# Values projected feature-major and transposed, last window rows staged in the product ring, and the last two down steps of every block taken token tile by token tile

## The chip, the cores and the metric

The kernel runs on one core of a Trainium2 chip. The metric is the device time of one execution in microseconds. Before the change it is 3422.22 us, the median of three runs (3419.22 to 3426.93). One further execution was profiled: 3422.57 us, with a span from its first to its last instruction of 3420.8 us. All times inside the kernel come from that execution.

## The reference, cut to what matters

One layer of a hybrid streaming encoder runs over a prompt of 2048 rows of width 1024 and over 32 further rows of a running stream (the sample):

```
h = rmsnorm(x, g_pre_mix)
[q | k | v | u_a | u_b | gate logits] = h @ w_in      # v: 2 heads of 64 = 128 columns
u = u_a * sigmoid(u_b)
attn = window attention (own chunk of 64 and two before, 16 query heads, 2 key/value heads, sinks, bias)
conv = silu(layernorm(causal depthwise conv of width 31 over u)) @ w_conv_out
m = sigmoid(g0) * attn + sigmoid(g1) * conv
x = x + rmsnorm(m @ w_out, g_post_mix)
h = rmsnorm(x, g_pre_ffn)
x = x + rmsnorm((silu(h @ w_gate) * (h @ w_up)) @ w_down, g_post_ffn)   # inner width 2816
```

Outputs are x for both streams, the last 128 rows of k and v of each stream, and the last 30 rows of u of each. All data is fp32. Every product of two fp32 operands is made of three matmuls of rounded parts: hi\*hi, hi\*lo and lo\*hi.

## The kernel before, in words

The prompt is cut into four **blocks** b of 512 tokens. The last block, where `ext(b)` holds, also carries the 32 sample rows, so it has 544 columns (two pieces of 272) and five token tiles in place of four. A block is a list of NS = 124 **steps** (`KINDS`), each with one 128x1024 weight tile in two parts: 16 GLU steps (0 to 15), 8 of q (16 to 23), k (24), v (25), 16 gates (26 to 41, `S_A` = 26), 8 of the convolution's projection (42 to 49), 8 of the output projection (50 to 57), 44 of the FFN (58 to 101) and 22 of the down projection (102 to 123, `S_D` = 102). `G(b, s)` numbers the steps over all blocks. TensorE goes through the steps in order and counts `w_used` up after each. Each other engine has its own loop over b and s in which step s mostly handles the result of step s - 1 (`r = s - 1`).

**Weights.** Rings of 3 slots for the high parts and 4 for the low parts are filled by the SyncE queue (SP). `load_hi(g)` waits until step g - 3 is used, `load_lo(g)` until step g - 4 is. In block 0 the parts are made on the spot (`split_hi` on ScalarE, `split_lo` on VectorE) and stored for the later blocks. SP's program is one ordered list: `weights_at`, then stores and loads of activations at fixed steps.

**Matmul forms.** `feature_major` holds a 128x128 weight tile and streams 512 tokens (24 matmuls; 48 of 272 tokens in the last block); its result is features by tokens. `token_major` with `token_products` holds a tile of tokens and streams 512 features. The v step has a form of its own, `values_of` (L830 to L843): it holds the tokens and streams the 128 value columns, in 96 matmuls of 128 columns (120 in the last block), so that values come out tokens by features, as `times_values` wants them. ScalarE then writes `v_hi` (L1241 to L1245) and VectorE `v_lo` (L1604 to L1610). In the last block VectorE also adds the high and low parts of the last keys and values into `kwin` and `kwin_s` (L1613 to L1622), which lie where `tmp` and `rs_bc` do; SP stores them at step 28 (`S_A + 2`, L603 to L608) and VectorE waits for these stores (L1639) before the layer norm.

**Convolution.** VectorE takes most taps (`conv`, L1388), accumulating in PSUM banks 4 to 7. For three channel tiles ScalarE makes products into the ring `prod` and GpSimd adds them (L692). Both start in a new block only when the previous block's rows are stored (`y_out`), since y shares memory with `x1`. After the taps come `channel_means` (L910), VectorE's subtraction of the mean (L1644), ScalarE's squares (L1261), `channel_squares` (L920) and the scaling (L1659). In blocks 1 to 3 the means follow step 26 and the squares step 27; in block 0 this lies three steps later. The attention units start at step 31 (34 in block 0). The probabilities' parts `pt_hi`, `pt_lo` share memory with `prod`.

**Down steps and the end of a block.** `f_hi` and `f_lo` have two slots. ScalarE makes the high part of down step dd when step dd - 2 is used (L1334 to L1336), VectorE the low part after it (L1756), and TensorE waits for `flo_ok`. After the last step ScalarE takes the squares of the second half of each token tile (`post_squares`, L1101 and L1113), GpSimd makes 1/rms (`post_inv_rms`, L662 to L665), and VectorE runs `residual` (L1435, L1440), which counts `pn_ok`. `store_y` issues one store of the block's rows when the last tile is done: in blocks 0 to 2 at SP's step 1 of the next block, in the last block at the very end, with a second store for the sample. At step 1 of the last block TensorE waits for the previous block's residual of tile 3, because that block uses banks 2 and 3 there.

The order within the down steps is set in TensorE's loop:

```
pe.wait_ge(flo_ok, b * FT + dd + 1)
token_major(b, s, S_D, f_hi[:, dd % 2], f_lo[:, dd % 2], (0, 1), HALF_D,
            range(tiles(b)))
```

## Time and profile before

| what | value |
|---|---|
| median of 3 runs | 3422.22 us (3419.22 to 3426.93) |
| profiled execution: time, span | 3422.57 us, 3420.8 us |
| TensorE busy | 3293.7 us, 96% |
| TensorE weight loads (beside the matmuls) | 2778.7 us, 81% |
| VectorE busy | 1551.4 us, 45% |
| ScalarE busy | 1062.5 us, 31% |
| GpSimd busy | 476.2 us, 14% |
| mean granted TensorE clock | 0.983 |
| data moved | 623.30 MB, 182 GB/s |

A matmul's listed duration is that of one from start to end, and neighbours overlap; what a step costs is the distance between starts. PE is TensorE, PEld its weight loads, DVE VectorE, ACT ScalarE, POOL GpSimd, SP SyncE. A wait in square brackets is the engine's idle time before the instruction and what released it.

### The profile page before, as it was taken

What the parts mean: (1) busy time and instruction counts of PE and PEld (TensorE: products, weight loads), DVE (VectorE), ACT (ScalarE), POOL (GpSimd) and SP (SyncE); (2) the same over time, 40 slices, a digit from 0 to 9 for tenths busy, and PEclk for the clock granted to TensorE, in tenths of its full rate; (3) what the DMA queues carried; (4) which work ended last, traced back from release to release, by engine and by line L of the source; (5) the groups of instructions that cost most, each with busy time, mean ns of one, the idle gap of its engine ahead of it and who ended that gap; (6) DMA issues with size and microseconds to landing.
All of it is one profiled execution on the core that took longest, in us unless ns stands there. A gap on an engine that the chain in (4) does not pass through costs nothing.

```text
span 3420.8 us, 43119 instructions
## 1 busy us (share of the span) xinstructions
PE 3293.7 (96%) x17118; PEld 2778.7 (81%) x17118; DVE 1551.4 (45%) x2779; ACT 1062.5 (31%) x1924; POOL 476.2 (14%) x515
## 2 busy tenths in 40 slices
PE   7999989999999999999999999999999998999997
PEld 6778768878787878888787888888898997899985
DVE  6966755544775541013695542003495555200012
ACT  3655432234345421003254421003153532200021
POOL 2830000000460000000280000000074000100000
PEclk9999999999999999999999999999999999999998
DMA  7764367777543355555553354555553322455542
GB/s 233 281 219 163 148 249 283 288 279 285 209 173 123 111 196 174 195 197 198 206 188 124 111 185 173 185 196 199 194 177 126 111 94 85 160 173 173 173 148 106
DMA packets 177895, 623.30 MB, mean 182 GB/s; under 512 B 20592, under 2 KB 28080, under 8 KB 177184
## 3 DMA queue, kind: packets, MB, share of 16 engines
q1 hardware_dynamic: 176736, 620.15, 51.6%
q8 instruction: 136, 2.23, 0.3%
q14 instruction: 63, 0.52, 0.0%
q10 hardware_dynamic: 960, 0.40, 0.0%
HBM read 481.13 MB, written 139.44 MB: 181 GB/s over the span
## 4 chain that ended last, share of the span: by engine, by line
PE 79%; DVE 3%; ACT 1%; DMA 1%; issue 1%; POOL 0%; SPq 0%; DVEq 0%; ACTq 0%; POOLq 0%
PE PS L747 49%; PE PS L801 6%; PE PS L803 6%; PE PS L802 6%; PE PS L783 2%; PE PS L873 2%; DVE PS L1388 1%; PE PS L861 1%; PE PS L920 1%; PE PS L862 1%; PE PS L863 1%; PE PS L890 1%; PE PS L891 1%; PE PS L731 1%; PE PS L892 1%
## 5 line engine op out<-in xcount | busy, mean ns | idle before, releaser
L747 PE MATMUL PS<-h_hi,w_hi 128*128 128x512 f32 (+1 forms) x3288 | 1053.6, 353 | 23.4 <-DVE u L1597 14.9
L747 PE MATMUL PS<-h_hi,w_lo 128*128 128x512 f32 (+1 forms) x3288 | 1054.6, 354 | 0.0
L747 PE MATMUL PS<-h_lo,w_hi 128*128 128x512 f32 (+1 forms) x3288 | 1043.6, 350 | 0.0
L747 PEld LDWEIGHTS PS<-h_hi,w_hi 128*128 128x128 f32 x3288 | 580.3, 189 | 106.4 <-issue 20.6
L747 PEld LDWEIGHTS PS<-h_lo,w_hi 128*128 128x128 f32 x3288 | 579.6, 189 | 89.7 <-issue 1.7
L747 PEld LDWEIGHTS PS<-h_hi,w_lo 128*128 128x128 f32 x3288 | 579.9, 189 | 80.9
L692 POOL TENSOR_TENSOR y<-y,prod 128x512 f32<-128x512 f32 (+1 forms) x333 | 407.9, 1251 | 228.4 <-ACT prod L1154 217.6
L1388 DVE SCALAR_TENSOR_TENSOR PS<-u,dw,PS 128x512 f32<-128x512 f32 (+1 forms) x604 | 434.4, 772 | 7.0
L1748 DVE TENSOR_TENSOR f<-PS,tmp 128x512 f32<-128x512 f32 (+1 forms) x88 | 61.6, 700 | 669.0 <-PE PS L747 650.2
L801 PE MATMUL PS<-w_hi,f_hi 128*128 128x512 f32 x748 | 297.4, 398 | 5.8 <-DVE f L1748 5.4
L803 PE MATMUL PS<-w_hi,f_lo 128*128 128x512 f32 x748 | 295.2, 395 | 0.0
L802 PE MATMUL PS<-w_lo,f_hi 128*128 128x512 f32 x748 | 294.0, 393 | 0.0
L1251 ACT ACTIVATE tmp<-PS 128x512 f32<-128x512 f32 (+1 forms) x88 | 52.9, 601 | 675.0 <-PE PS L747 655.7
L662 POOL TENSOR_TENSOR prs<-pss 128x1 f32<-128x1 f32 x34 | 11.1, 326 | 1790.7 <-ACT tmp L1113 1790.7
L1154 ACT ACTIVATE prod<-u,dw 128x512 f32<-128x512 f32 (+1 forms) x333 | 229.5, 730 | 34.5 <-POOL y L692 34.1
L1043 ACT ACTIVATE w_hi<-w_raw 128x1024 fp32r<-128x1024 f32 x124 | 131.3, 1059 | 349.9 <-DVE w_raw L1527 109.4
L1533 DVE TENSOR_TENSOR w_lo<-w_raw,w_hi 128x1024 fp32r<-128x1024 f32 x124 | 162.2, 1308 | 165.4 <-ACT w_hi L1043 164.9
L1756 DVE TENSOR_TENSOR f_lo<-f,f_hi 128x1024 fp32r<-128x1024 f32 (+1 forms) x88 | 109.1, 1240 | 271.3 <-ACT f_hi L1336 271.3
L1459 DVE CUSTOM_DVE_ANT_0 p<-PS,bias,sink_sb 128x256 f32<-128x256 f32 x272 | 115.6, 481 | 145.5 <-PE PS L873 141.9
L1336 ACT ACTIVATE f_hi<-f 128x1024 fp32r<-128x1024 f32 (+1 forms) x88 | 93.8, 1070 | 262.8 <-PE PS L803 262.8
L801 PEld LDWEIGHTS PS<-w_hi,f_hi 128*128 128x128 f32 x748 | 141.0, 189 | 38.6 <-DVE f L1748 7.0
L803 PEld LDWEIGHTS PS<-w_hi,f_lo 128*128 128x128 f32 x748 | 140.8, 188 | 33.4
(185 smaller groups left out, 4001.0 us busy)
## 6 DMA issues: line engine op xcount, KB each, us to landing
w_lo<-lo_dram SPq DMA_DIRECT2D x372, 512.0 KB, 4.5
w_hi<-hi_dram SPq DMA_DIRECT2D x372, 512.0 KB, 3.6
w_raw<-in_w_stream SPq DMA_DIRECT2D x124, 512.0 KB, 4.0
hi_dram<-w_hi SPq DMA_DIRECT2D x124, 512.0 KB, 4.1
lo_dram<-w_lo SPq DMA_DIRECT2D x124, 512.0 KB, 4.0
x<-in_x_prompt SPq DMA_DIRECT2D x4, 2048.0 KB, 11.4
out_y_prompt<-x SPq DMA_DIRECT2D x4, 2048.0 KB, 7.1
xs<-in_x_prompt SPq DMA_DIRECT2D x12, 512.0 KB, 5.5
```

The lines of the kernel that those rows point to most:

```text
L692: nc.gpsimd.tensor_tensor(y[:, ct, 0:yw], y[:, ct, 0:yw], prod[:, n % RING, 0:yw], ALU.add).then_inc(prod_used, 1)
L747: last = nc.tensor.matmul(PS[:, k0 + off, 0:n], w, x[:, k, c0:c0 + n], start=first and k == 0, stop=stop and k == KT - 1)
L801: nc.tensor.matmul(out, hi, wk[0], start=first, stop=False)
L802: nc.tensor.matmul(out, hi, wk[1], start=False, stop=False)
L803: return nc.tensor.matmul(out, lo, wk[0], start=False, stop=last_k)
L1043: A(w_hi[:, g % HI, :], w_raw[:, g % LO, :], ACT.Copy).then_inc(w_hi_ok, 1)
L1154: A(prod[:, n % RING, 0:yw], u[:, ct, k:k + yw], ACT.Copy, scale=dw[:, ct, k:k + 1]).then_inc(prod_ok, 1)
L1336: A(f_hi[:, dd % 2, :, 0:c], f[:, 2 * kp:2 * kp + 2, 0:c], ACT.Copy).then_inc(fhi_ok, 1)
L1388: ins = STT(out, src, dw[:, ct, k:k + 1], acc(b, ct), ALU.mult, ALU.add)
L1459: nc.vector.tensor_tensor_reduce(out=p[:, h, :], in0=PS[:, 2 + h // 2, (h % 2) * 2 * P:(h % 2 + 1) * 2 * P], in1=bias[:, head, :], scale=1 ...
L1533: TT(w_lo[:, g % LO, :], w_raw[:, g % LO, :], w_hi[:, g % HI, :].bitcast(F32), ALU.subtract).then_inc(w_lo_ok, 1)
L1756: TT(f_lo[:, dd % 2, :, 0:c], f[:, 2 * kp:2 * kp + 2, 0:c], f_hi[:, dd % 2, :, 0:c].bitcast(F32), ALU.subtract).then_inc(flo_ok, 1)
```

## The change

Three parts. **Values:** step 25 becomes a `feature_major` step. ScalarE copies its result to `tmp[:, 1]` (new semaphore `v_sb_ok`); after step 26 (`turn_step`) TensorE turns it by one 128x128 transpose per token tile into banks 6 and 7 (`turn_values`, `vt_done`), and `v_hi` and `v_lo` are made from there, one step later than before. In the last block the transposes stand behind the wait for all taps, ahead of the means. TensorE's step 27 waits for `v_sb_ok`, and the squares for `v_lo`. **Windows:** `kwin` and `kwin_s` move to the memory of the product ring. VectorE writes them once all products are used, one step later; the wait for their stores moves from VectorE's layer norm to ScalarE's second attention unit. SP's step for the stores stays 28. **Down steps:** `down_tail` takes steps 122 and 123 together, for each token tile both; each tile but the last counts `d_done`, and `post_squares` waits for its tile alone. Both steps' `w_used` come with the last tile. In the last block `store_y` makes one store per token tile. Shown without unchanged surroundings:

```diff
 ckv = at("ckv", R_pt, [P, 2, P])
-kwin = at("kwin", R_sc, [P, 2, P])
-kwin_s = at("kwin_s", R_sc + 2 * P * 4, [P, 2, P])
+kwin = at("kwin", R_pt, [P, 2, P])
+kwin_s = at("kwin_s", R_pt + 2 * P * 4, [P, 2, P])
 assert top[0] <= nc.sbuf_usable_end, (top[0], nc.sbuf_usable_end)
...
 o_done, w_gain_ok = sem("o_done"), sem("w_gain_ok")
+d_done = sem("d_done")
...
 kv_hi_ok, hist_ok = sem("kv_hi_ok"), sem("hist_ok")
+v_sb_ok, vt_done = sem("v_sb_ok"), sem("vt_done")
 dve_chain, pool_chain, act_chain = sem("dve_chain"), sem("pool_chain"), sem("act_chain")
...
+
+def turn_step(b):
+
+    return S_A
...
     def store_y(b):
-        m = post_tile(b, tiles(b) - 1, 1)
-        sp.wait_ge(pn_ok, m + 1)
+        if ext(b):
+            for tt in range(4):
+                sp.wait_ge(pn_ok, post_tile(b, tt, 1) + 1)
+                r0 = b * T + tt * P
+                sp.dma_start(y_prompt[r0:r0 + P, :], x1[:, tt, :]).then_inc(y_out, 16)
+            sp.wait_ge(pn_ok, post_tile(b, 4, 1) + 1)
+            sp.dma_start(y_sample, x1[SR:P, 4, :]).then_inc(y_out, 16)
+            return
+        sp.wait_ge(pn_ok, post_tile(b, tiles(b) - 1, 1) + 1)
         sp.dma_start(y_prompt[b * T:(b + 1) * T, :].rearrange("(t p) d -> p t d", p=P),
                      x1[:, 0:4, :]).then_inc(y_out, 16)
-        if ext(b):
-            sp.dma_start(y_sample, x1[SR:P, 4, :]).then_inc(y_out, 16)
...
                 sp.dma_start(u[:, :, HIST + T:UW - S], state).then_inc(state_in, 16)
-            if ext(b) and s == S_A + 2:
+            if ext(b) and s == turn_step(b) + 2:
                 sp.wait_ge(win_ok, 4)
...
     store_y(NB - 1)
-    sp.wait_ge(y_out, 16 * (NB + 1))
+    sp.wait_ge(y_out, 16 * (NB - 1 + 5))
     sp.wait_ge(win_out, 16 * 8)
...
             result_out(pe, b, s - 1)
-        result_out(pe, b, s - 2)
+        if s == S_A + 1:
+            pe.wait_ge(v_sb_ok, b + 1)
+        else:
+            result_out(pe, b, s - 2)
         for k in range(KT):
...
-    def values_of(b, s):
-
-        g, k0 = G(b, s), zbank(b, s)
-        weights(g)
-        result_out(pe, b, s - 2)
+    def down_tail(b):
+
         for tt in range(tiles(b)):
-            t0, out = tok0(b, tt), PS[:, k0 + tt // 4, (tt % 4) * P:(tt % 4 + 1) * P]
-            for k in range(KT):
-                hi, lo = h_hi[:, k, t0:t0 + P], h_lo[:, k, t0:t0 + P]
-                wk = [w[:, g % n, k * P:(k + 1) * P] for w, n in ((w_hi, HI), (w_lo, LO))]
-                nc.tensor.matmul(out, hi, wk[0], start=k == 0, stop=False)
-                nc.tensor.matmul(out, hi, wk[1], start=False, stop=False)
-                last = nc.tensor.matmul(out, lo, wk[0], start=False, stop=k == KT - 1)
-        last.then_inc(w_used, 1)
+            for s in (NS - 2, NS - 1):
+                dd = s - S_D
+                if tt == 0:
+                    weights(G(b, s))
+                    pe.wait_ge(flo_ok, b * FT + dd + 1)
+                for kk in range(2):
+                    last = token_products(b, s, S_D, f_hi[:, dd % 2], f_lo[:, dd % 2], (0, 1), HALF_D,
+                                          kk, tt)
+                if tt == tiles(b) - 1:
+                    last.then_inc(w_used, 1)
+            if tt < tiles(b) - 1:
+                last.then_inc(d_done, 1)
+
+    def turn_values(b):
+
+        pe.wait_ge(v_sb_ok, b + 1)
+        for tt in range(tiles(b)):
+            last = nc.tensor.transpose(PS[:, 6 + tt // 4, (tt % 4) * P:(tt % 4 + 1) * P],
+                                       tmp[:, 1, tok0(b, tt):tok0(b, tt) + P], ident_sb[:])
+        last.then_inc(vt_done, 1)
...
             if s < first_unit(b):
-                if s == S_A - 1:
-                    values_of(b, s)
-                elif b or s >= 2:
+                if b or s >= 2:
                     feature_major(b, s, h_hi, h_lo, groups(b))
+                if s == turn_step(b):
+                    if ext(b):
+                        pe.wait_ge(conv_step, taps_before(b + 1))
+                    turn_values(b)
                 ln = s - S_A - ln_shift(b)
...
                 if ln == 3 and ext(b):
-                    pe.wait_ge(conv_step, taps_before(b + 1))
                     channel_means(b, ypieces, (0, 2, 4, 1, 3, 6, 7, 5), True, True)
                 if ln == 4:
+                    result_out(pe, b, S_A - 1)
                     channel_squares(b, ypieces)
...
                     pe.wait_ge(hf_ok, first_norm(b + 1, tiles(b + 1) - 1) + 1)
+                if s >= NS - 2:
+                    if s == NS - 1:
+                        down_tail(b)
+                    continue
                 pe.wait_ge(flo_ok, b * FT + dd + 1)
...
             if kind == "v":
-                zv = PS[:, zbank(b, r), :].rearrange("p (t a d) -> p t a d", t=4, a=2)
+                A(over(b, tmp[:, 1, 0:c]), z(b, r), ACT.Copy).then_inc(v_sb_ok, 1)
+            if r == turn_step(b):
+                act.wait_ge(vt_done, b + 1)
                 if ext(b):
-                    zw = PS[:, zbank(b, r) + 1, 0:P].rearrange("p (a d) -> p a d", a=2)
-                    A(v_hi[:, 5, 0:3:2, :], zw, ACT.Copy)
-                A(v_hi[:, 1:5, 0:3:2, :], zv, ACT.Copy).then_inc(kv_hi_ok, 1)
+                    A(v_hi[:, 5, 0:3:2, :], PS[:, 7, 0:P].rearrange("p (a d) -> p a d", a=2), ACT.Copy)
+                A(v_hi[:, 1:5, 0:3:2, :], PS[:, 6, :].rearrange("p (t a d) -> p t a d", t=4, a=2),
+                  ACT.Copy).then_inc(kv_hi_ok, 1)
             if kind == "gate":
...
                 for n in units_at(b, s):
+                    if n == 1 and ext(b):
+                        act.wait_ge(win_out, 16 * 6)
                     if 0 < n <= units(b):
...
                     sum_squares(b + 1, start, 0)
-        act.wait_ge(w_used, G(b, NS - 1) + 1)
         for tt in range(tiles(b)):
+            if tt < tiles(b) - 1:
+                act.wait_ge(d_done, out_tile(b, tt))
+            else:
+                act.wait_ge(w_used, G(b, NS - 1) + 1)
             post_squares(b, tt, 1)
...
             kind = KINDS[r] if r >= 0 else None
-            if kind in BY_DVE:
+            if kind in BY_DVE and kind != "v":
                 dve.wait_ge(w_used, G(b, r) + 1)
...
                    ALU.subtract).then_inc(z_dve, 1)
-            if kind == "v":
+            if r == turn_step(b):
                 dve.wait_ge(kv_hi_ok, 2 * b + 2)
                 if ext(b):
-                    zw = PS[:, zbank(b, r) + 1, 0:P].rearrange("p (a d) -> p a d", a=2)
+                    zw = PS[:, 7, 0:P].rearrange("p (a d) -> p a d", a=2)
                     TT(v_lo[:, 5, 0:3:2, :], zw, v_hi[:, 5, 0:3:2, :].bitcast(F32), ALU.subtract)
-                zv = PS[:, zbank(b, r), :].rearrange("p (t a d) -> p t a d", t=4, a=2)
+                zv = PS[:, 6, :].rearrange("p (t a d) -> p t a d", t=4, a=2)
                 TT(v_lo[:, 1:5, 0:3:2, :], zv, v_hi[:, 1:5, 0:3:2, :].bitcast(F32),
...
-                    dve.wait_ge(z_dve, by_dve(b, r))
+                    dve.wait_ge(z_dve, by_dve(b, S_A - 1))
+                    dve.wait_ge(prod_used, adds)
                     for o, hi, lo in (
...
                     nc.vector.tensor_copy(u_new[:], u[:, :, UW - HIST:UW]).then_inc(u_saved, 1)
-                    dve.wait_ge(win_out, 16 * 6)
                 dve.wait_ge(mu_done, b + 1)
```

## Rows read from the trace of the kernel before

**Rows 1.** The page, part 1: busy time, share of the span, instructions.
```profile
PE 3293.7 (96%) x17118; PEld 2778.7 (81%) x17118; DVE 1551.4 (45%) x2779; ACT 1062.5 (31%) x1924; POOL 476.2 (14%) x515
```
**Rows 2.** Waits of PE, starts of blocks 1 and 3: total us, times, longest.
```profile
PE PS L747 <- DVE u L1597: 3.0, 2, 2.8
PE PS L747 <- DVE x L1440: 6.7, 1, 6.7
```
**Rows 3.** Step 25 in blocks 1, 3: window; us, PE busy, clock, DMA, GB/s.
```profile
1010.90:1021.50 10.60, 10.60 (x98) 1.00 0.01 2
2602.70:2616.00 13.30, 13.30 (x122) 1.00 0.23 80
```
**Rows 4.** Chain that ended last: eight transposes, step 26 of blocks 1, 3: start, us.
```profile
490.17 0.89 PE PS L731 x8
...
1021.58 5.58 PE PS L747 x24
...
2616.05 6.07 PE PS L747 x48
```
**Rows 5.** Timeline of block 0 around the start of step 25: start, us.
```profile
183.09 0.40 PE L747 MATMUL PS<-h_hi,w_lo 128*128 128x512 f32 x1
...
189.41 0.68 DVE L1602 TENSOR_TENSOR k_lo<-PS,k_hi 128x512 fp32r<-128x512 f32 x1
```
**Rows 6.** Timeline around step 25: last taps of blocks 1, 3; ACT's values.
```profile
1011.91 0.75 DVE L1388 SCALAR_TENSOR_TENSOR y<-u,dw,PS 128x512 f32<-128x512 f32 x1
...
2608.37 0.81 DVE L1388 SCALAR_TENSOR_TENSOR y<-u,dw,PS 128x574 f32<-128x574 f32 x1
...
1021.62 0.60 ACT L1245 ACTIVATE v_hi<-PS 128x512 fp32r<-128x512 f32 x1 [12.53 <-PE PS L842]
```
**Rows 7.** Chain that ended last, block 3, means to squares: start, us.
```profile
2622.12 8.57 PE PS L910 x32
2630.69 6.12 PE PS L747 x48
...
2639.14 3.42 DMA out_v_win_s<-kwin_s
...
2644.13 11.25 PE PS L920 x32
```
**Rows 8.** Timeline of DVE in block 3: the mean's subtraction.
```profile
2642.57 5.66 DVE L1644 TENSOR_TENSOR y<-y,PS 128x512 f32<-128x512 f32 x16 [23.26 <-DMA out_v_win_s<-kwin_s]
```
**Rows 9.** Start of block 3, columns as in rows 3: wait, then step 1.
```profile
2449.40:2456.10 6.70, 0.03 (x1) 0.88 0.46 157
2456.10:2464.70 8.60, 8.60 (x50) 0.70 0.73 258
```
**Rows 10.** Timeline of block 1's start: first matmul, store, first tap, second GLU.
```profile
864.93 0.39 PE L747 MATMUL PS<-h_hi,w_hi 128*128 128x512 f32 x1
...
877.76 0.40 SPq L569 DMA_DIRECT2D out_y_prompt<-x  x1
...
885.21 0.81 DVE L1383 TENSOR_SCALAR PS<-u,dw,gn 128x512 f32<-128x512 f32 x1 [6.55 <-DMA out_y_prompt<-x]
...
894.64 0.68 DVE L1597 TENSOR_TENSOR u<-PS,tmp 128x512 f32<-128x512 f32 x1
```
**Rows 11.** Timeline of block 0, step 122: first matmul, last low part.
```profile
853.83 0.39 PE L801 MATMUL PS<-w_hi,f_hi 128*128 128x512 f32 x1
...
855.25 1.23 DVE L1756 TENSOR_TENSOR f_lo<-f,f_hi 128x1024 fp32r<-128x1024 f32 x1 [3.27 <-ACT f_hi L1336]
```
**Rows 12.** Timeline of the kernel's end: last matmul, first and last residual.
```profile
3397.46 0.40 PE L803 MATMUL PS<-w_hi,f_lo 128*128 128x512 f32 x1
...
3399.79 0.75 DVE L1435 SCALAR_TENSOR_TENSOR ostash_d<-ostash_d,prs,gp 128x512 f32<-128x512 f32 x1 [13.26 <-POOL prs L665]
...
3412.11 1.30 DVE L1440 TENSOR_TENSOR x<-x,PS 32x512 f32<-32x512 f32 x2
```
**Rows 13.** DMA issues: size, median us to landing.
```profile
xs<-in_x_sample SPq DMA_DIRECT2D x1, 128.0 KB, 3.3
```

## The prediction, made before the changed kernel ran

> **What bounds the kernel now.** I read the page first: TensorE is busy for 96% of the span and every other engine for less than half [rows 1]. So only three things count: columns that TensorE need not stream, places where it stands still, and what runs after its last matmul. Next, its waits: in the window of block 1's start two waits for VectorE's u of 3.0 us together (the window of block 2's start answers with the same row), in that of block 3's start one of 6.7 us for a residual [rows 2]. Then the windows and the chain around step 25 and around the last block's layer norm [rows 3, 4, 7], and the timelines of the engines that would have to keep up [rows 5, 6, 8, 10, 11]. Last, the end: the last matmul starts at 3397.46 and takes 0.40 us, so 3420.8 - 3397.86 = 22.9 us of the span have no TensorE work [rows 12].
>
> The sum is made against the profiled execution (3422.57 us, span 3420.8). It lies 0.35 us above the median of the three runs, too little to matter. About 0.2%, 7 us, is what a measurement of this kernel can tell from no change.
>
> **A. The v step.** Today step 25 takes 10.6 us in blocks of 512 and 13.3 us in the last, at granted clock 1.00 [rows 3]: 96 and 120 matmuls of 128 columns, 111 ns each. A feature-major step takes 5.58 us (24 matmuls, 0.23 us each) and 6.07 us (48 of 272) [rows 4]. Saved: 3 x 5.0 + 7.2 = 22.2 us. The count of streamed columns is the same before and after in blocks 0 to 2, and the time is not: at 128 columns a matmul is paced by something other than its columns.
>
> Against this speaks a rule of the Trainium skill ("TensorE: Matmul & The Clock Gate", section Back-to-back issue gap): N/2.4 + 2.5 ns for an isolated matmul of N columns, 56 ns at 128. By it step 25 would cost 5.4 us now, feature-major 5.2, and part A would lose its gain. The trace's 111 ns disagrees, and the measurement decides.
>
> Added to TensorE: four transposes per block, five in the last, 17 in all. Eight take 0.89 us [rows 4], so 0.11 each, 1.9 us; I add 0.15 us per block for entering and leaving them: 2.5 us. Bounds: nothing added at the edges, 1.9, and twice the row, 3.8, if they run as the first of a group do. They wait for ScalarE's copy, which is made during step 26, when ScalarE was idle for 12.53 us before its v copy [rows 6]; without that cover each wait would be one 0.60 us copy. The copy to `v_hi` moves to step 27 and VectorE's `v_lo` with it. The mean matmuls cover both in blocks 1 to 3. The four window additions, a few tenths each, also fall there. GpSimd's last adds end with the products and before the means; I charge nothing for VectorE's new wait on them. The first work queued behind that wait is the mean's subtraction, which needs those adds anyway.
>
> What the long step covered: VectorE's lag. In block 1 its last tap starts at 1011.91 and the step ends at 1021.5; in block 3 they are at 2608.37 and 2616.0 [rows 3, 6]. With step 25 five to seven us shorter, the taps are needed only after step 26, at about 1021.8 and 2614.7, so there is room. In block 0 VectorE also splits weights and is late: k_lo starts at 189.41 and takes 0.68, while step 25 starts at about 183.4 [rows 5] and would now end near 188.9. Step 26 needs k_lo: TensorE waits 1.2 us. That takes 1.2 back. **A = -22.2 + 2.5 + 1.2 = -18.5 us.**
>
> **B. The window stores in the last block.** Today VectorE stands 23.26 us until the last of the four stores has landed [rows 8]. SP issues these only after step 27 has freed weight slots, at 2636.8, so TensorE finishes step 27 and has no squares until 2644.13. The squares then take 11.25 us, where 16 matmul pairs of the same shape for the means took 8.57 [rows 7]. From the end of step 27 to the end of the squares it is 18.6 us. Without the wait the subtraction (5.66 us) starts when the means end, at 2630.69, and is over within step 27 (6.12 us). The squares follow at once; I take 9.0 us, the means' row and 0.4 for ScalarE's pace. The stores leave VectorE's path; ScalarE waits for them at the second unit, four steps later, some 24 us after their issue against 3.42 us for the last one's landing: nothing. If that cover were gone, softmax and all behind it would wait. **B = 9.0 - 18.6 = -9.6 us**, bounds -7.3 (the pause alone) and -10.0.
>
> **C. Starts of blocks 1, 2 and 3.** Today the first matmul of block 1 starts at 864.93, the residuals end when SP issues the store at 877.76, the store lands, and VectorE's first tap starts at 885.21, 20.3 us after the block's start [rows 10]. With the tail, three of four tiles are done before the last matmul. The last tile needs squares and 1/rms (1.9 us from the last matmul's end to the first residual) and one residual of about 2.7 us (five in 13.6 us, 3399.79 to 3413.4) [rows 12]: done at +4.7 us, where it was +12.8. SP is at its step 1 when step 0 is used, +5.6, issues two weight loads and then the store at +6.4, which lands 7.4 later: first tap at +13.9, some 6.4 us sooner. The second GLU tile, 9.4 us behind the first tap [rows 10], is ready at +24.0 and needed by step 5 at +27.7. Both waits of 3.0 us go. What is late next is nothing on TensorE, by a margin of 3.7 us. At block 3 the wait for tile 3 (ready at +4.7, wanted at +6.0) goes: 6.7 us [rows 2]. Step 1 behind it took 8.60 us at granted clock 0.70 after a stretch at 0.88 [rows 9], where 48 such matmuls take 6.07 at clock 1.00 [rows 4]: 2.5 us more, part of it at the 1.2 GHz level, which goes too. The state's load stands behind the store on SP; it lands near +15, and step 3 needs its result at +18. **C = -3.0 - 3.0 - 6.7 - 2.5 = -15.2 us.**
>
> **D. The end.** Five residuals in a row become one. From the last matmul: 1.9 us to the last residual, 2.7 us for it, +4.7; tile 3's ends at +1.9. SP issues five stores instead of two; four are under way by then. The last has 128 KB. Its landing: at least the 3.3 us of the load of the same size [rows 13], at most what the last stores take today, 3420.8 - 3413.4 = 7.4. I take 3.8, near the low end, since only one 512 KB store runs beside it. 8.5 in place of 22.9: **D = -14.4 us**, bounds -14.9 and -10.8.
>
> **E. What the tail costs.** Matmul count and form stay. But step 123's products come after six matmuls instead of 24. The last low part is made during step 122: the step starts at 853.83, VectorE's f_lo starts at 855.25 and takes 1.23 [rows 11], ready at +2.65. TensorE wants it at +1.4. It waits 1.25 us in every block, queue and all: **E = +5.0 us**, bounds 0 (if the copy comes early enough) and +8 (if the two weight slots, now freed together, are late for the next block as well). Weights for block b+1's step 1 are asked for 1.4 us before the end and needed 5.6 after it; I charge them nothing.
>
> **Sum:** -18.5 - 9.6 - 15.2 - 14.4 + 5.0 = -52.7 us; 3422.6 - 52.7 = 3369.9, I say **3370 us**. TensorE's idle time and columns carry 43 of it, the end 14.
>
> **The rivals.**
> 1. *The starts keep their waits.* The store still stands behind two weight loads on SP, and four further loads are asked for around the block's end. If store and loads share the queue so that the store lands no earlier, C's part for blocks 1 and 2 goes, and with a late state load block 3 waits at step 3 instead of step 1. For: the store is the release of the first tap [rows 10]. Against: it is issued 6.4 us sooner. All of C lost: 3370 + 15.2 = 3385.
> 2. *The layer norm of block 3 stays late.* Some other wait replaces the stores', such as ScalarE's `v_hi` copies or VectorE's wait for the products. Against: both are over before the means end. Price 9.6: 3380.
> 3. *The values part gives nothing*: transposes and new waits eat it, or 128-column matmuls cost only their columns. By a rate of 0.23/4 us for 128 columns, A would be its transposes and the k_lo wait alone, +3.7: 3370 + 22 = 3392. By the skill's rule above it would be near this too. The 111 ns of this trace speak plainly against it.
> 4. *Slower.* One mechanism: both weight slots of the down tail come free only with the last tile, and four loads of 512 KB, the 2 MB store and the next loads meet at every block's start. A 2 MB store takes 7.4 us here [rows 10], so four weight loads would too: 1.4 us before the end plus 7.4 is +6.0, 0.4 us too late for step 1. To end above the old time by 0.2% this must cost 52.7 + 7 = 60 us, 20 us at each of three boundaries; it decides only if loads land some 15 to 20 us late, with steps at the lower clock behind the pauses. Then: 3430. The ring has two steps of slack, so this is remote.
>
> That an edit does not do what it says: the old waits are taken out of the program text, so only their successors can bring them back, which are rivals 1 and 2.
>
> **How the numbers follow.** My forecast 0.78; rival 1 0.08; rival 2 0.06; rival 3 0.03; rival 4 and anything like it 0.02; the rest, 0.03, lies on the fast side (E not paid, more of the unit phase freed). Within the forecast the bounds of A, B, D and E give about -7 and +7, and the runs scatter by -3 to +5. The range 3359 to 3385 takes these in, with rival 2 and half of rival 1. Faster by over 0.2%: 0.97; within 0.2%: 0.01; slower: 0.02.
>
> **What would show it.** Right if in the profile after: no matmul of 128 columns at step 25, a step of about 5.6 us there, and 17 transposes of about 0.11 us; no VectorE idle time for a window store, squares starting with the end of step 27; no TensorE wait for a residual at block 3 and step 1 at clock 1.00; a pause of about 1.25 us for f_lo inside each tail; and 8 to 9 us from the last matmul to the end. Wrong if TensorE waits for taps before the transposes, for u at blocks 1 to 3, for weights at a block's second step, or if the last store lands far later than 4 us.

## The result, and the profile after the change

The changed kernel takes 3370.87 us (median of 4 runs, 3362.13 to 3372.42), the kernel before beside it 3421.99 us (4 runs, 3419.22 to 3426.93). The ratio is 0.9844, with a 95% interval of 0.9832 to 0.9857: 51 us or 1.6% faster, 0.9 us from the forecast of 3370.0. The profiled execution of after took 3371.6 us, span 3369.8.

Part 1 of the page of after answers to [rows 1]:

```profile
PE 3269.2 (97%) x16847; PEld 2751.1 (82%) x16847; DVE 1553.7 (46%) x2779; ACT 1064.4 (32%) x1928; POOL 475.1 (14%) x515
```

TensorE has 271 instructions and 24.5 us of busy time fewer. The span is 51.0 us shorter, so about half of the gain is matmul time that is no longer there (the narrow matmuls and the slow ones), and half is idle time and the end.

The chain that ended last in after, start and us. First block 1 from the means over step 25 to the squares, then block 3 from the means to the squares (answering to [rows 7]):

```profile
1002.71 4.29 PE PS L933 x10
1007.01 11.05 PE PS L761 x48
1018.49 2.58 PE PS L933 x6
...
2598.71 8.57 PE PS L933 x32
2607.29 6.12 PE PS L761 x48
2613.41 8.57 PE PS L943 x32
2621.98 6.14 PE PS L761 x48
```

Steps 25 and 26 together are 48 matmuls in 11.05 us, where step 25 alone took 10.6 [rows 3]. What filled the narrow form can be seen in the windows of before, step 25 and then step 26 of block 1 (us, then busy time of PE, PEld, DVE, ACT and POOL, granted clock, DMA share, GB/s):

```profile
1010.90:1021.50 10.60, 10.60 (x98) 10.60 (x97) 1.68 (x3) 0.00 (x0) 0.78 (x1) 1.00 0.01 2
1021.60:1027.10 5.50, 5.50 (x25) 4.48 (x25) 0.88 (x2) 0.60 (x1) 0.00 (x0) 1.00 0.53 191
```

There is one weight load per matmul in both, listed with 0.19 us each. In the narrow form the loads leave no gap (10.60 of 10.60 us); in the wide form they fill 4.48 of 5.50. That fits the loads as what paces the narrow matmuls, but no run shows it.

In after, the gap from 1018.06 to 1018.49, 0.43 us, is the four transposes. In block 3 the three stages stand end to end: the squares begin when step 27 ends. The instructions of the transposing line show that all 17 exist and have one shape (their 272 ns are the latency of one; four of them together took those 0.43 us):

```profile
L864 PE MATMUL PS<-ident_sb,tmp x17: 270/272/273, 199.6 to 2598.4; 128*128 128x128 f32 x17
```

VectorE's timeline in block 3, answering to [rows 8]: the mean's subtraction no longer stands 23.26 us behind a store, and its wait is one for the means.

```profile
2607.32 5.65 DVE L1680 TENSOR_TENSOR y<-y,PS 128x512 f32<-128x512 f32 x16 [5.37 <-PE PS L933]
```

What TensorE waited for in after (total us, times, longest), the rows that the change touches:

```profile
PE PS L761 <- DVE u L1633: 8.3, 6, 6.0
...
PE PS L815 <- DVE f_lo L1792: 5.1, 4, 1.4
...
PE PS L761 <- DVE u L1630: 2.4, 1, 2.4
PE PS L761 <- DVE k_lo L1638: 2.2, 1, 2.2
```

The wait for the residual [rows 2] is gone. The 5.1 us for f_lo are term E as priced. Of the 8.3 us for u, 7.4 lie in block 0 and 0.2 and 0.7 in blocks 1 and 2, where [rows 2] had 3.0 each. The row for L1630 is new. It is in block 3. A wait for u in blocks 1 to 3 stood among the prediction's signs of being wrong, and all three blocks have one: 0.2, 0.7 and 2.4 us. SP's timeline of the starts of blocks 1 and 3, and VectorE's behind them:

```profile
870.65 0.42 SPq L582 DMA_DIRECT2D out_y_prompt<-x  x1
...
2438.99 0.43 SPq L582 DMA_DIRECT2D out_y_prompt<-x  x1
2439.47 0.64 SPq L613 DMA_DIRECT2D u<-in_state  x1
```
```profile
881.29 0.81 DVE L1419 TENSOR_SCALAR PS<-u,dw,gn 128x512 f32<-128x512 f32 x1 [4.95 <-DMA out_y_prompt<-x]
...
2451.66 0.44 DVE L1627 TENSOR_TENSOR u<-PS,tmp 128x272 f32<-128x272 f32 x1 [7.16 <-DMA u<-in_state]
```

The store of block 1 is issued 6.6 us after the block's first matmul (864.09), where it was 12.8 [rows 10]: the prediction had 6.4. But it takes 10.6 us to land in place of 7.4, so the first tap starts at +17.2 and not at +13.9. The windows from the store's issue to its landing, before and then after, say what it met:

```profile
877.76:885.20 7.44, 7.44 (x34) 6.05 (x34) 0.86 (x2) 0.60 (x1) 0.00 (x0) 1.00 0.89 318
870.65:881.26 10.61, 10.61 (x48) 8.67 (x47) 0.98 (x2) 0.41 (x1) 0.00 (x0) 1.00 0.98 344
```

The store's own 2048 KB are 282 GB/s of the 318 and 198 of the 344. What runs beside it went from about 36 to 146 GB/s, with the DMA engines at 98%.

In block 3 the 120 KB state load, issued 0.48 us behind the 2 MB store, takes 12.1 us to land. Windows of block 3's start (us, PE, PEld, DVE, ACT, POOL busy, granted clock, DMA share, GB/s) show what the queue was doing:

```profile
2431.91:2444.10 12.19, 12.19 (x98) 12.19 (x97) 5.07 (x8) 2.60 (x4) 0.93 (x3) 1.00 0.82 281
2444.10:2450.10 6.00, 6.00 (x49) 5.91 (x47) 0.28 (x1) 0.00 (x0) 0.00 (x0) 1.00 1.04 384
2450.10:2452.60 2.50, 0.13 (x2) 0.00 (x0) 0.85 (x3) 0.62 (x1) 0.00 (x0) 1.00 1.03 377
```

Before, the stretches from +6 us on moved 157 and 258 GB/s [rows 9]; now store, state and weights meet at 377 to 384 with the DMA engines full. The granted clock stays at 1.00 (2.4 GHz) through the pause, where it was 0.88 and then 0.70 with the pause of 6.7 us before. That holds for this execution. In that of after_again, the same kernel, the clock is at the lower level for nearly all of the 3.6 us behind the same pause (us, PE busy, clock, DMA share, GB/s):

```profile
2455.44:2459.00 3.56, 3.56 (x16) 0.52 0.53 208
```

The end, VectorE's and SP's timelines, answering to [rows 12]:

```profile
3353.12 0.75 DVE L1471 SCALAR_TENSOR_TENSOR ostash_d<-ostash_d,prs,gp 128x512 f32<-128x512 f32 x1 [3.73 <-POOL prs L676]
...
3364.65 1.45 DVE L1471 SCALAR_TENSOR_TENSOR PS<-PS,prs,gp 32x512 f32<-32x512 f32 x2
3366.13 1.30 DVE L1476 TENSOR_TENSOR x<-x,PS 32x512 f32<-32x512 f32 x2
```
```profile
3356.00 8.98 SPq L577 DMA_DIRECT2D out_y_prompt<-x  x4
3367.47 0.33 SPq L579 DMA_DIRECT2D out_y_sample<-x  x1
```

The last matmul ends at 3362.33. Four residuals are by then done or under way, the last starts 2.3 us later, and the span ends 7.5 us after the matmul (22.9 before).

### The profile page after: what moved, and what is told of

It is laid out like the page before. It is cut to its first block, busy times and chain, and to the rows that moved or that the text cites. A ratio compares the mean times of both kernels' runs of the same rounds, so it can differ in the third digit from the quotient of the medians.

```text
span 3369.8 us, 42601 instructions
## 1 busy us (share of the span) xinstructions
PE 3269.2 (97%) x16847; PEld 2751.1 (82%) x16847; DVE 1553.7 (46%) x2779; ACT 1064.4 (32%) x1928; POOL 475.1 (14%) x515
## 4 chain that ended last, share of the span: by engine, by line
PE 80%; DVE 2%; ACT 2%; DMA 1%; issue 1%; POOL 0%; SPq 0%; DVEq 0%; ACTq 0%; POOLq 0%
PE PS L761 50%; PE PS L815 7%; PE PS L817 6%; PE PS L816 6%; PE PS L797 2%; PE PS L896 2%; DVE PS L1424 1%; PE PS L884 1%; PE PS L885 1%; PE PS L913 1%; PE PS L886 1%; PE PS L914 1%; PE PS L915 1%; PE PS L742 1%; PE PS L943 1%
## 5 line engine op out<-in xcount | busy, mean ns | idle before, releaser
L761 PE MATMUL PS<-h_hi,w_hi 128*128 128x512 f32 (+1 forms) x3328 | 1065.5, 353 | 16.4 <-DVE u L1633 8.3
L761 PE MATMUL PS<-h_hi,w_lo 128*128 128x512 f32 (+1 forms) x3328 | 1065.6, 353 | 0.0
L761 PE MATMUL PS<-h_lo,w_hi 128*128 128x512 f32 (+1 forms) x3328 | 1055.5, 350 | 0.0
L673 POOL TENSOR_TENSOR prs<-pss 128x1 f32<-128x1 f32 x34 | 10.1, 298 | 1747.8 <-ACT tmp L1142 1747.6
```

The costliest lines, as they stand in the source:

```text
L761: last = nc.tensor.matmul(PS[:, k0 + off, 0:n], w, x[:, k, c0:c0 + n], start=first and k == 0, stop=stop and k == KT - 1)
```

## A ledger of stretches

Medians of a whole run say how much a part is worth; the places of a few matmuls say where. For every kernel I took the first matmul of blocks 1 and 3, the end of block 3's squares (where the next step's first matmul starts) and the end of the last matmul from TensorE's timeline, and the starts of the means (x10 in block 1, x32 in block 3) and of block 1's squares (x16) from the chain. The differences, in us:

```
kernel             block 1 start  block 1 means  block 3 start  block 3 means     after last
                   to means       to squares     to means       to squares' end   matmul
before             141.7          28.6           178.9          33.1              22.9
only_windows       143.9          28.6           178.2          23.1              22.9
tail_last_block    144.0          28.6           178.3          33.5               7.5
only_tail          138.8          28.6           172.1          33.3               7.5
values_one_store   142.9          23.9           170.9          32.5              22.9
only_values        142.8          23.9           170.2          32.8              17.9
no_tail_one_store  142.5          23.9           170.3          23.1              22.9
after              138.6          23.9           166.8          23.1               7.5
after_again        139.6          23.9           166.3          23.1               7.5
low_part_hidden    138.6          23.9           167.4          23.1               8.2
state_first        138.6          23.9           163.2          23.1               7.5
all_three          139.4          23.9           164.0          23.1               8.2
all_three_again    138.5          23.9           164.1          23.1               8.2
```

Each column has two to five levels, and which level a kernel stands on goes with its edits. Within a level the values lie within 1.1 us, in the first column within 2.3. Each row is one execution. What lies outside these stretches is not so steady: block 0 took 858.8 to 870.2 us over all kernels, and from block 3's squares to the last matmul 737 to 747. So a single span says little to within 5 us, and each part below is judged by its column and by the medians.

## The experiments

The parts were tried alone first; each ran beside the kernel before, and each ratio is against it.

**only_values.** The change's values (feature-major step 25, transposes, copies moved) and the kernel before in the rest. The core of the edit, against after:

```diff
-        kwin = at("kwin", R_pt, [P, 2, P])
+        kwin = at("kwin", R_sc, [P, 2, P])
...
-                        if s >= NS - 2:
-                            if s == NS - 1:
-                                down_tail(b)
-                            continue
...
+                act.wait_ge(w_used, G(b, NS - 1) + 1)
...
+                            dve.wait_ge(win_out, 16 * 6)
```

> The kernel before with the values part alone (feature-major step 25, copy, transposes, v_hi and v_lo a step later). My account: three steps 5.0 us shorter and one 7.2, 2.5 us of transposes, 2.2 us of TensorE waiting for k_lo in block 0: 17.5 us less than before, near 3404.5 us, with VectorE's wait for the window stores and all start waits still there. Rival (the values part gives nothing, the gain sits elsewhere): within 4 us of the kernel before, 3418 to 3426.

Measured: 3395.31 us (4 runs, 3392.49 to 3398.14), ratio 0.9916 [0.9904, 0.9929]. That is 9 us under the expectation, and part of the miss is my own: this kernel also kept the last block's stores split by token tile, which the expectation did not count. After the last matmul it takes 17.9 us where before has 22.9. It was therefore run again with one store (values_one_store, below). Its wait for k_lo was 0.6 us.

**only_windows.** The staging place alone, with the wait that goes with it (VectorE's for the products) and the new place of the wait for the stores; everything of the values, the tail and the split stores as before. The core, against the kernel before:

```diff
-        kwin = at("kwin", R_sc, [P, 2, P])
+        kwin = at("kwin", R_pt, [P, 2, P])
...
+                            if n == 1 and ext(b):
+                                act.wait_ge(win_out, 16 * 6)
...
+                            dve.wait_ge(prod_used, adds)
...
-                            dve.wait_ge(win_out, 16 * 6)
```

> The kernel before with only the windows moved to the product ring's memory (VectorE's wait for their stores gone, ScalarE's in its place). My account: the squares of block 3 start at the end of step 27 and take 8.6 us, 10 us less, and 1.5 us less in the first unit's step behind it, where the granted clock was 0.84: near 3411 us. Rival (another wait takes the stores' place, the layer norm of block 3 stays late): 3420 to 3423 us, squares still about 18 us behind the end of step 27.

Measured: 3415.82 us (7 runs, 3410.85 to 3419.31), ratio 0.9975 [0.9965, 0.9985], 7.9 us by the medians (before 3423.71). Its chain, start and us:

```profile
2628.06 8.57 PE PS L910 x32
2636.63 6.11 PE PS L747 x48
2642.74 8.57 PE PS L920 x32
```

The squares begin as step 27 ends and last exactly as long as the means. From the means' start to the squares' end it is 23.1 us, 10.0 under before: term B was -9.6 with the squares taken at 9.0. The first unit's step behind took 7.72 us before, at a granted clock of 0.78, and takes 6.25 here, so the 1.5 us that the expectation had for it are there too. The median is all the same 5 us above the expected 3411: the interval, 5 to 12 us, holds both, and the medians don't settle the size.

**only_tail.** The last two down steps token tile by token tile in every block and the split stores, with the values and the window staging of before. The core, against the kernel before:

```diff
+            def down_tail(b):
...
+                        if s >= NS - 2:
+                            if s == NS - 1:
+                                down_tail(b)
+                            continue
...
-                act.wait_ge(w_used, G(b, NS - 1) + 1)
                 for tt in range(tiles(b)):
+                    if tt < tiles(b) - 1:
+                        act.wait_ge(d_done, out_tile(b, tt))
+                    else:
+                        act.wait_ge(w_used, G(b, NS - 1) + 1)
```

> The kernel before with only the last two down steps taken tile by tile and the last block's stores split. My account: the end 15.5 us shorter, the starts of blocks 1 and 2 shorter by 2.8 and 2.3 us, that of block 3 by 6.8 (6.7 of wait and 2.5 of slow step less 2.4 of a new wait for the state's load), 5.1 us of new waits for f_lo: 22 us less, near 3400 us. Rival (starts keep their waits, because store and weight loads crowd the queue): only the end and the f_lo waits count, 10.4 us less, 3411.5 us. Rival (both weight slots come free too late): TensorE waits for weights at the second step of blocks 1 to 3, more than 3405 us.

Measured: 3398.5 us (6 runs, 3396.6 to 3407.35), ratio 0.9929 [0.9917, 0.9941], 25.2 us under before. Its waits:

```profile
PE PS L753 <- DVE u L1626: 10.0, 7, 5.9
PE PS L807 <- DVE f_lo L1785: 5.1, 4, 1.4
PE PS L753 <- DVE u L1623: 1.0, 1, 1.0
```

The f_lo waits are there with no part of A or B beside them, so they belong to the tail alone. Rival 4's late weight slots have no row at the block starts.

**tail_last_block.** The same, but the new order only in the last block. Against only_tail:

```diff
-                        if s >= NS - 2:
+                        if ext(b) and s >= NS - 2:
                             if s == NS - 1:
                                 down_tail(b)
```

> As only_tail, but blocks 0 to 2 keep the old order of steps 122 and 123; only the last block goes tile by tile. My account: the end 15.5 us shorter, one f_lo wait of 1.3 us, starts of blocks 1 to 3 as before: 14.2 us less, near 3408 us. If the starts of blocks gained nothing in only_tail, this kernel would be faster than only_tail by three f_lo waits, 4 us; by my account it is 8 us slower than only_tail.

Measured: 3408.68 us (5 runs, 3404.45 to 3411.74), ratio 0.9956 [0.9944, 0.9967]: 15.0 us under before and 10.2 above only_tail. It has one f_lo wait of 1.4 us, and the wait of the block start is back:

```profile
PE PS L753 <- DVE x L1471: 6.7, 1, 6.7
```

So C (block starts, less three f_lo waits) and D (the end) are separate gains: 10 us and 15 us. The profiled spans of the two kernels, 3402.5 and 3402.6, do not show it, because block 0 was 8 us shorter in this one and the last block's gate and up steps 3.3 us; the ledger and the medians do.

**values_one_store.** only_values with the last block's output stored as before. Against only_values:

```diff
-                        sp.dma_start(y_prompt[r0:r0 + P, :], x1[:, tt, :]).then_inc(y_out, 16)
...
+                if ext(b):
+                    sp.dma_start(y_sample, x1[SR:P, 4, :]).then_inc(y_out, 16)
```

> The values' change alone, this time with the last block's output stored as before (one 2 MB store and the sample rows' store at the end), which the kernel only_values did not keep. Theory: the time after the last matmul goes from the 17.96 us of only_values back to 22.9 us, and the rest stays, so 3395.3 + 5.0 = about 3400 us, 22 us under the kernel before; the values' term by itself is then 3.5 us larger than the 18.5 us that the prediction took. Rival 1: the term is 18.5 us and the rest of only_values was scatter between executions: 3403 to 3404 us. Rival 2: splitting the store brings nothing by itself: 3395 us and 18 us after the last matmul.

Measured: 3401.04 us (5 runs, 3399.59 to 3407.41), ratio 0.9941 [0.9929, 0.9953], 21.8 us under before (3422.82). The time after the last matmul is back at 22.9. So splitting the store brings 5 us even with the residuals in one row at the end, a third of D. What remains, 21.8, is 3.3 above the 18.5 of term A, but its interval, 16 to 24 us, holds both. In the ledger, block 1's way from the means to the squares is 4.7 us shorter (A per block of 512: 5.0 - 0.6 = 4.4), block 3's from its start to the means 7.3 to 8.7 (7.2 - 0.7 = 6.5). The second has a part that is not A's. Windows of block 3's pause of 6.7 us and of the 8.6 us behind it, in this kernel (columns as above), answering to [rows 9]:

```profile
2438.40:2445.10 6.70, 0.03 (x2) 0.02 (x1) 6.53 (x11) 0.62 (x1) 0.31 (x1) 0.70 0.45 158
2445.10:2453.70 8.60, 8.60 (x58) 8.60 (x59) 0.29 (x1) 0.00 (x0) 0.00 (x0) 0.84 0.78 263
```

The same pause, but the granted clock behind it is 0.84 on average instead of 0.70, and 58 matmuls run in it instead of 50, at 0.126 us each 1.0 us sooner. All three kernels with the new values and the old block starts show this (0.83 or 0.84), all three with the old values and starts 0.69 or 0.70. The low stretch lies earlier against the pause: in the pause itself the clock is 0.70 on average where it was 0.88, and over both windows together it is 0.78 in either kernel. The same loss falls more on the idle time, where it costs nothing. What sets where it falls is open, and with one execution of each kernel that it is the edit's doing is not shown. With that part, blocks 1 to 3 give 2 x 4.7 + 8.0 = 17.4 us; block 0 lies in the scatter and would need 4.4 to make 21.8.

**no_tail_one_store.** Values and windows together, tail and stores as before:

```diff
-                        if s >= NS - 2:
-                            if s == NS - 1:
-                                down_tail(b)
-                            continue
...
+                act.wait_ge(w_used, G(b, NS - 1) + 1)
```

> The values' and the windows' change together, without the token-tile-by-token-tile down steps and without the split store: the last steps of every block, the block starts and the end as before. Theory (the parts add): the whole change's 3371 us and the 24 to 25 us that the tail brought alone, about 3395 us; the squares of block 3 last 8.6 us and begin at the end of step 27, and the waits for u at the block starts are those of before (3, 3 and 6.7 us). Rival (the tail is worth less beside the values' change, since the 2 MB store now lands 10.6 to 11.0 us after its issue and eats the margin at the starts): 3388 to 3391 us.

Measured: 3393.18 us (6 runs, 3389.87 to 3405.99), ratio 0.9922 [0.9908, 0.9936]. The windows' part beside the values' is 7.9 us again. The tail's part beside both is 3393.2 - 3370.9 = 22.3 us, where it was 25.2 alone. The DMA issues of this kernel (KB, median us to landing), and the same row in after:

```profile
out_y_prompt<-x SPq DMA_DIRECT2D x4, 2048.0 KB, 7.1
u<-in_state SPq DMA_DIRECT2D x1, 120.0 KB, 8.7
```
```profile
out_y_prompt<-x SPq DMA_DIRECT2D x3, 2048.0 KB, 11.0
```

Issued 12.8 us into the block the 2 MB store lands in 6.8 to 7.7 us; issued 6.6 to 7.1 us into it, it takes 10.6 to 12.0 in after. The column of block 3's start shows where the tail's worth went: alone it takes 6.4 us from it (178.5 on the mean of three to 172.1), beside the values' change 3.7 to 4.2 (170.5 to 166.8 in after and 166.3 in after_again). Two things fill the gap of 2.4. The slow matmuls that the pause of 6.7 us brings, and that go with it, cost 1.0 us less in the executions with the new values, as above. And the state's load lands 10.7 us after its issue in only_tail and 12.1 in after, so the wait for it is 1.0 there and 2.4 here. With the state loaded first (below) the column is at 163.2 to 164.1, where both parts added up put it (178.5 - 8.0 - 6.4 = 164.1).

**after_again, state_first, low_part_hidden, all_three.** Four kernels on one chip, to take out one by one the three waits that after still has. after_again is the changed kernel itself. state_first issues the state load ahead of the store:

```diff
-                    if s == 1 and b:
-                        store_y(b - 1)
                     if s == 1 and ext(b):
                         sp.wait_ge(w_used, G(b, 0))
                         sp.dma_start(u[:, :, HIST + T:UW - S], state).then_inc(state_in, 16)
+                    if s == 1 and b:
+                        store_y(b - 1)
```

low_part_hidden gives TensorE two tiles of step 122 before the first of step 123:

```diff
+                order = [(0, 0), (0, 1), (1, 0), (1, 1)] + [(k, tt) for tt in range(2, tiles(b)) for k in range(2)]
+                for k, tt in order:
+                    s = NS - 2 + k
...
```

all_three has both, and VectorE's k_lo ahead of its split of the weights' low part:

```diff
-                    if not S_F <= s < S_D - 2:
-                        split_lo(G(b, s) + 2)
...
+                    if not S_F <= s < S_D - 2 and kind != "k":
+                        split_lo(G(b, s) + 2)
...
+                        split_lo(G(b, s) + 2)
```

> The changed kernel once more, unaltered, as the base of this group and to see how far its stages scatter between executions. Both theories: 3362 to 3373 us, near 3371; block 0 within 4 us of the first profile, the waits for f_lo (5.1 us), k_lo (about 2 us) and the state's load (2.4 us) there again.

> The changed kernel with SP issuing the last block's state load ahead of the store of block 2's rows. My theory: in block 3 the first GLU tile waited for the state, whose 120 KB stood behind the 2 MB store in the same queue (12.1 us to landing). The load should now land within 8 us and TensorE's wait of 2.4 us at step 3 go: 2.4 us less than the changed kernel. Rival: the queue as a whole is full there (four weight loads and two more), so the state is late in front of the store too: no change, landing still over 10 us.

> The changed kernel with the tail in the order tile 0 and tile 1 of step 122, then tiles 0 and 1 of step 123, then each further tile as before, so that twelve matmuls (2.8 us) stand ahead of step 123's first use of f_lo. My theory: the four waits for f_lo, 5.1 us, go and nothing is lost, since tile 0 is done 1.4 us later but VectorE's residuals still end with the last tile: 5 us less. Rival: the f_lo waits gave the residuals and the weight loads time that they need, so the wait returns at the start of the next block or at the end: 0 to 2 us less.

> The changed kernel with the state load first, the f_lo waits hidden, and k_lo made ahead of the split of step 27's weights on VectorE (for the 2.2 us that TensorE waited for k_lo in block 0). If all three waits were real ends of the path, about 9.5 us less than the changed kernel, near 3361 us; if the waits only stood in for others, less than 5 us.

> The change with the three repairs once more (state loaded ahead of the store, two tiles of the one-before-last step ahead of the last step's low part, k_lo ahead of the split of w_lo), to see whether its median holds. Theory: 3362 to 3368 us, some 5 us under the change's own 3371 to 3373 us, of which the state load has 3 us, the low part's waits 5 us and k_lo at most 2 us, less what two further waits of the order of 1 us take back. Rival: the 3365.3 us were a lucky sample, and it stands at the change's 3371 us.

Measured, with before at 3422.28 us in the first four rows and 3422.82 in the last:

```
kernel            median us  range               ratio   95% interval       L1630 wait  f_lo waits  k_lo wait
after_again       3373.46    3365.78 to 3380.61  0.9858  0.9843 to 0.9873   2.3         5.1         0.7
state_first       3368.22    3363.34 to 3374.50  0.9839  0.9825 to 0.9852   none        5.1         0.6
low_part_hidden   3366.93    3365.26 to 3373.51  0.9843  0.9829 to 0.9856   2.9         none        0.6
all_three         3365.34    3361.10 to 3367.29  0.9833  0.9820 to 0.9846   none        none        none
all_three_again   3363.61    3361.28 to 3373.09  0.9833  0.9819 to 0.9847   none        none        none
```

Each wait goes with its edit and stays without it, so the three causes are shown. The k_lo wait is 0.6 to 0.7 us here and not the 2 us expected from after's one profile. State: the DMA issues of state_first (KB, median us to landing), and VectorE's first use of it:

```profile
u<-in_state SPq DMA_DIRECT2D x1, 120.0 KB, 6.7
```
```profile
2446.31 0.44 DVE L1627 TENSOR_TENSOR u<-PS,tmp 128x272 f32<-128x272 f32 x1 [1.30 <-DMA u<-in_state]
```

It lands in 6.7 us instead of 12.1, and block 3's column is at 163.2 to 164.1 us with the edit and 166.3 to 167.4 without: 3 us. Low part: blocks 1 and 2, first matmul to first matmul, take 781.2 to 783.1 us in the three kernels with the edit and 782.6 to 787.0 in the three without, 2.4 us per block by their means (the six values of either side: 782.3 against 784.7; the f_lo wait itself is 1.3). The two groups overlap, so that more than the wait comes back isn't settled. The end gives 0.7 us back: 8.2 us after the last matmul in place of 7.5, since the first tiles are done later. All three together: the medians are 5 to 10 us under the changed kernel's two (3370.9 and 3373.5). The intervals still touch, so that it is faster is likely, and the size not settled. The expectation of 9.5 us under, if all three waits were ends of the path, or less than 5, if they were not, is not decided by them either. Against before it is 0.983, the best of the study.

## Why the prediction was right, and where it was off

Its signs first. No 128-column matmuls are left at step 25, the transposes take 0.11 us each, the squares begin with the end of step 27, the wait for the residual is gone, and the f_lo pauses are 1.24 to 1.36 us. The end, 7.5 us, is shorter than the 8 to 9 named. One sign of being wrong came true, the waits for u in blocks 1 to 3 (3.3 us together), and it belongs to term C.

**A, -18.5: mechanism right, size 2 to 3 us low.** Steps and transposes came out as written (4.4 per block predicted, 4.7 measured; transposes 0.43 us for four). Step 25 cost 111 ns per matmul at 128 columns [rows 3] and now costs what any feature-major step costs. The formula of the Trainium skill for an isolated matmul ("TensorE: Matmul & The Clock Gate", section Back-to-back issue gap), 56 ns at 128 columns, by which this part had nothing to give, does not describe these matmuls. The same section warns of that: for a stream in which every matmul has its weight load it puts about 81 ns. The 111 ns of this trace lie above that figure too. The k_lo wait was 2.2 us in one execution and 0.6 to 0.7 in all other kernels that have it; 1.2 was taken. Block 3's way to the means gained 8.0 where 6.5 was taken, 1.0 of it from a higher clock behind a pause that A does not touch. Blocks 1 to 3 together gave 17.4 by the ledger where 15.3 was taken; block 0 can't be told from its scatter.

**B, -9.6: right.** 10.0 by the ledger (9.4 beside the new values), 7.9 by the medians in both surroundings. The squares' row was the means' row, 8.57, without the 0.4 added for ScalarE. The 11.25 us before came at a granted clock of 0.78.

**C, -15.2: the step that failed is "which lands 7.4 later".** The issue time was right to 0.2 us. But the duration of 7.4 was read where only about 36 GB/s ran beside the store, and the same edit moved it into the stretch where weight loads are asked for, with some 146 GB/s beside it. It took 10.6 us, so the margin of 3.7 us was eaten: waits of 0.2 and 0.7 us are left at blocks 1 and 2, nearly nothing. In block 3 the same error hit the state's load, "lands near +15, and step 3 needs its result at +18". It landed at +19.7 and TensorE waited 2.4 us. This is rival 1's mechanism at a fraction of its price; state_first shows it. What C lost there it partly won back: block 1's start to means went from 143.0 (mean of the six kernels with the old tail, 141.7 to 144.0) to 138.9 (mean of the seven others), 4.1 less where 3.0 was counted. No row tells what the extra 1 us is. By the medians C comes to 22.3 - 15.4 + 5.1 = 12.0 us beside the other parts, 3.2 under its price.

**D, -14.4: right, 15.4.** The last store's 128 KB landed within about 2 us of its issue (1.9 in the DMA issues) where 3.8 was taken from a load.

**E, +5.0: right in its waits** (5.1), though blocks 1 and 2 may give back more than that, about 2.4 us each in low_part_hidden and its like, when they go.

**The sum.** Alone the parts bring 21.8, 7.9 and 25.2 us, 54.9 together, and the whole change 51.1: what is missing is the interaction at block 3's start, 2.4 us, and scatter (the interval of each part is 3 to 4 us to either side). Against the prediction the medians give values 21.8 (18.5), windows 7.9 (9.6) and the tail beside both 22.3 (24.6): errors of +3.3, -1.7 and -2.3 us that cancel. The 0.9 us between forecast and result is luck; each term was known to 2 or 3 us.

**The rivals.** 2 and 3 are excluded by only_windows and values_one_store, 4 by only_tail. Of 1 about 3 us of 15 came true.

## What to carry to other kernels

A transfer that is moved earlier must be priced by the traffic it moves into, not by its duration where it stood; and in one queue a small load that somebody waits for goes ahead of a large store that nobody needs yet. Where matmuls with a fresh weight tile each are narrow, look at the time of one before counting columns: making the result in the wide form and turning it with a few transposes cost 11.48 us here where narrow matmuls cost 16.2 (the means' end to their second part in block 1, step 26's 5.6 in both). When the two last stages share their result, finish it tile by tile, with enough work in front of the operand that is made last, and store each tile as it is done.

## What the runs showed of the hardware that was not expected

A 2 MB store took 6.6 us to land at the kernel's end with only the sample's 128 KB beside it, 6.8 to 7.7 us when issued about 13 us into a block (318 GB/s with the rest in block 1 of before), and 10.1 to 12.3 us when issued 6.5 to 8 us into one (344 GB/s in block 1 of after). A 120 KB load took 6.1 to 6.7 us ahead of such a store. Right behind it, it took 7.1 to 8.7 us in the quiet stretch and 10.7 to 12.5 in the full one.

2016 matmuls of 272 columns from the last block's gate and up steps have the same code everywhere. In the chain they take 254.24 us in most executions and 250.89 in others, the granted clock at 1.00 in both (before, then only_values):

```profile
2988.84 254.24 PE PS L747 x2016
```
```profile
2967.07 250.89 PE PS L761 x2016
```

126.1 and 124.4 ns each; after and values_one_store had 253.14 and 253.13. The rate holds through the whole stretch in each. It goes with no edit: low_part_hidden, only_values and tail_last_block had the fastest one. Differences of this size between single executions are no evidence for or against a change.
